# Decoder trunk on one core: the identity products between stages are left out

## The chip, the cores and the metric

The kernel runs on one NeuronCore of one Trainium2 chip. The metric is device time in microseconds (us) of that core, the median of repeated runs. Lower is better.

## The reference

Two layers work on two groups of tokens that share one set of weights: a prompt of 16 meta tokens and 256 prompt tokens, and eight sample sequences of eight tokens. That makes 336 token columns, and the model width is 1024. Each layer has three sub-layers:

```
x = x + 0.5 * rms_norm(swiglu(rms_norm(x, g0), gate1, up1, down1), g1)
x = x +       rms_norm(mixer(rms_norm(x, g2), ...),               g3)
x = x + 0.5 * rms_norm(swiglu(rms_norm(x, g4), gate2, up2, down2), g5)
```

The mixer joins a gated delta-rule head group (four heads of 128) and a short gated convolution into one output projection. All arithmetic is 32-bit floating point. Both a sub-layer's input and its output are normalised, so nothing of the next sub-layer can be multiplied before the output's norm is known and the sum with x has been made.

## The kernel before, in words

Everything is kept features first: a tile holds 128 features on the partitions and up to 336 tokens along the row, and x is eight such tiles. A weight block of 128x128 is split into a high part WH (ScalarE, L710) and a low part WL (VectorE, L1003), x likewise into XH (ScalarE, L727) and XL (VectorE, L1015). Each product of the model is therefore three TensorE products of 336 columns: WH with XH, WH with XL, WL with XH. The helper `three` (L1437 to L1439) issues them; `entry` issues its own (L1477, L1478, L1482). Weights come by DMA into three slots from the sync queue.

The five engines' programs are written by hand, each one a plain sequence, joined by semaphores. A layer is FFN (j = 0), mixer (j = 1), FFN (j = 2). Between two of them lies a hand-over, on which four engines work in turn:

- TensorE, `out_norm(layer, j)`: sums the squares of the output over the features with columns of ones. L1574 does it for the tiles summed so far, L1577 for the last tile. After that it waits for y_inv and spreads the inverse root over the partitions with three transposes (L1455).
- ScalarE takes the root (L767).
- VectorE takes the reciprocal (L1051) and, once TensorE's rows are there, scales the eight output tiles (L1058) and adds them to x (L1064).
- ScalarE then makes XH from each new tile of x (L727), VectorE XL (L1015).
- TensorE's `entry` begins as soon as XH of tile 0 stands. Its first three parts use tiles 0, 1 and 2 of x for three outputs each: 27 products. The rest follow as the tiles come.

The norm of the new x is not needed before the first outputs are read. Its column sums (L1462) stand among TensorE's products, ScalarE takes the root (L752), VectorE the reciprocal (L1027), TensorE spreads it (L1455 again), and VectorE copies it (L1029) and scales the first outputs (L1101, L1102). The products of the third chunk after them wait for that.

There are six hand-overs, the last of them at the end of the program with no stage behind it. In the first five, `out_norm` also calls `keep_busy(n)`: n products of the 128x128 identity with itself into columns of bank 6 of PSUM that nobody reads (L1569). They are issued without a wait of their own. A call with n = 4 (n = 2 for j = 1) stands between L1577 and the wait for y_inv, and a call with n = 7 behind L1455. A 32-bit product of this kind is two passes, each with a weight load, so it makes two records in the profile. At the start of the program 14 products on a blank tile (L1833) are issued in the same way, while the first data are on their way; the change does not touch those.

Of the kernel before, what the change touches and what calls it, by code (L numbers as in the profile page):

```python
# [22 lines left out]
P = 128  # L23
DEPTH = 2
# [228 lines left out]
def decoder_trunk(nc, io):  # L253
    ctx = ExitStack()
    with ctx:
# [16 lines left out]
        def stack(at, *specs):  # L272
            out = []
            for name, shape, dt in specs:
# [47 lines left out]
        (NI, MI), e_end = stack(h_at, ("NI", [P, TT, HEADS, P], F32), ("MI", [P, TT, HEADS, P], F32))  # L322
        (EXT,), at = stack(e_end - size([P, 2 * HEADS, G_LEN]), ("EXT", [P, QKV_T, G_LEN], F32))
        (OH, _, OL), _ = stack(at, ("OH", [P, HEADS, TP], F32R), ("OV", [P, HEADS, TP], F32),
                                  ("OL", [P, HEADS, TP], F32R))
        (QKV, UEXT, ZS, BY, QKM), at = stack(
# [31 lines left out]
        PS = ctx.enter_context(nc.psum_tensor("PS", [P, 8, 512], F32))  # L358
# [56 lines left out]
        def mask(name, width=P):  # L415
            return MK[:, MASKS.index(name), 0:width]
# [59 lines left out]
        def tcols(t):  # L476
            return slice(t * P, (t + 1) * P)
# [516 lines left out]
        def _(dve):  # L994
# [198 lines left out]
            def mixer(layer):  # L1193
                for step in STEPS:
# [81 lines left out]
                    elif what == "mirror":  # L1276

                        _, t, m = step
                        own(("y", t, m), layer)
                        if m < SQUARE:  # L1280
# [5 lines left out]
                        ins.then_inc(mirrored.sem, 1)  # L1286
                    elif what == "x":
                        _, t, m = step
                        group(step, layer)
                        name = "lv8_meta" if t == C_TILE and m == 8 else f"lv{m}"  # L1290
# [143 lines left out]
        def _(pe):  # L1434
# [17 lines left out]
            def rows(col, out):  # L1452

                for t in range(TT):
                    ins = pe.transpose(out[:, tcols(t)], col[:, t:t + 1].to_broadcast([P, P]), mask("ident"))  # L1455
                return ins
# [106 lines left out]
                for m in range(KT):  # L1563
                    down_tile(m)

            def keep_busy(n):

                for _ in range(n):
                    pe.matmul(PS[:, 6, 0:P], mask("ident"), mask("ident"), start=True, stop=True)  # L1569

            def out_norm(layer, j):
                pe.wait_ge(y_acc.sem, y_acc.at(j * (KT - 1) + KT - 2, layer))
                for t in range(TT):
                    pe.matmul(Y_COLS[:, t:t + 1], ACCY[:, tcols(t)], mask("ones", 1), start=(t == 0), stop=False)  # L1574
                pe.wait_ge(y_sq.sem, y_sq.at(j * KT + KT - 1, layer))
                for t in range(TT):
                    ins = pe.matmul(Y_COLS[:, t:t + 1], SQY[(KT - 1) % 2][:, tcols(t)], mask("ones", 1), start=False,  # L1577
                                    stop=(t == TT - 1))
                ins.then_inc(y_cols.sem, 1)
                last = (layer, j) == (DEPTH - 1, 2)  # L1580
                if not last:
                    keep_busy(2 if j == 1 else 4)
                pe.wait_ge(y_inv.sem, y_inv.at(j, layer))
                rows(RC[:, 1, :], Y_ROWS).then_inc(y_rows.sem, 1)
                if not last:
                    keep_busy(7)

            def evacuated(name, layer):

# [244 lines left out]
            for layer in range(DEPTH):  # L1834
                ffn(layer, 0)
                out_norm(layer, 0)
                mixer(layer)
                out_norm(layer, 1)
                ffn(layer, 1)
                out_norm(layer, 2)  # L1840
# [96 lines left out]
```

## Time and profile before

| | us |
|---|---|
| median of 3 runs | 1436.12 |
| lowest and highest run | 1435.62, 1437.96 |
| time of the profiled execution | 1436.65 |
| its span, first to last instruction | 1434.8 |
| TensorE, busy in the span | 1413.1 |
| mean granted clock of TensorE | 0.997 |

The span is what the profile's views divide up; 1.85 us of the profiled execution lie around it. The profiled execution is 0.53 us above the median. In the profile, PE is TensorE's products and PEld its weight loads. A product's end is modelled, so products that follow each other closely overlap in the rows: the distance from start to start is the pace, and the duration of one is longer than that.

### The profile page before, as it was taken

To read this page: it belongs to the slowest core of one execution; us is meant where nothing else is said; L and a number is where in the kernel's file an instruction comes from. 1 tells how busy PE (TensorE), PEld (TensorE's weight loads), DVE (VectorE), ACT (ScalarE), POOL (GpSimd) and SP (SyncE) were. 2 spreads that over 40 slices of the span, in tenths; PEclk is the share of its full clock that TensorE was granted. 3 is DMA by queue.
4 is the path that set the end of the run, shared out by engine and by line. 5 is a ranking of instruction groups with operands and counts; after the bars stand their busy time and mean duration, and the time that the engine had idled before them with its cause. 6 is when DMAs were issued, how large, how long until landed. Compare 5 with 4: busy or idle time off the path is not lost.

```text
span 1434.8 us, 22786 instructions
## 1 busy us (share of the span) xinstructions
PE 1413.1 (98%) x9588; PEld 1397.8 (97%) x9588; DVE 880.0 (61%) x1486; ACT 625.1 (44%) x978; POOL 37.3 (3%) x124
## 2 busy tenths in 40 slices
PE   8999999999999999999999999999999999999997
PEld 8999999899999999999999999998999999999997
DVE  5655533798697765553376555348986967655433
ACT  5444333572444444433344443336734345444332
POOL 0000000110000000000000000001100000000000
PEclk9999999999999999999999999999999999999998
DMA  6544344322116344434435443442221253444442
GB/s 225 208 147 147 120 142 162 107 89 89 65 60 207 115 136 140 146 122 145 163 126 193 137 145 128 144 166 92 89 89 64 71 203 118 149 155 148 138 144 98
DMA packets 49605, 191.17 MB, mean 133 GB/s; under 512 B 6144, under 2 KB 8576, under 8 KB 48992
## 3 DMA queue, kind: packets, MB, share of 16 engines
q1 hardware_dynamic: 48896, 184.60, 38.5%
q0 software_dynamic: 608, 5.12, 0.9%
q8 instruction: 76, 1.25, 0.3%
q14 instruction: 25, 0.20, 0.0%
HBM read 183.27 MB, written 6.43 MB: 132 GB/s over the span
## 4 chain that ended last, share of the span: by engine, by line
PE 91%; DVE 6%; ACT 2%; issue 0%; DMA 0%; SPq 0%; ACTq 0%
PE PS L1437 26%; PE PS L1438 26%; PE PS L1439 26%; PE PS L1608 3%; DVE WL L1003 2%; PE PS L1716 1%; PE PS L1705 1%; PE PS L1477 1%; PE PS L1482 1%; PE PS L1478 1%; ACT XH L727 1%; DVE XL L1015 1%; PE PS L1738 1%; PE PS L1606 1%; DVE X L1064 1%; PE PS L1649 1%
## 5 line engine op out<-in xcount | busy, mean ns | idle before, releaser
L1437 PE MATMUL PS<-XH,WH 128*128 128x336 f32 (+1 forms) x1728 | 550.3, 318 | 2.6 <-DVE WL L1003 2.0
L1439 PE MATMUL PS<-XH,WL 128*128 128x336 f32 (+1 forms) x1728 | 542.3, 314 | 0.0
L1438 PE MATMUL PS<-XL,WH 128*128 128x336 f32 (+1 forms) x1728 | 541.9, 314 | 0.0
L1003 DVE TENSOR_TENSOR WL<-RAW,WH 128x1024 fp32r<-128x1024 f32 (+1 forms) x312 | 398.1, 1300 | 195.4 <-ACT WH L710 195.3
L710 ACT ACTIVATE WH<-RAW 128x1024 fp32r<-128x1024 f32 (+1 forms) x312 | 345.4, 1120 | 255.8 <-DMA RAW<-in_w_down 172.5
L1437 PEld LDWEIGHTS PS<-XH,WH 128*128 128x128 f32 x1728 | 324.7, 188 | 4.2 <-issue 2.9
L1438 PEld LDWEIGHTS PS<-XL,WH 128*128 128x128 f32 x1728 | 324.8, 188 | 0.3
L1439 PEld LDWEIGHTS PS<-XH,WL 128*128 128x128 f32 x1728 | 324.3, 188 | 0.0
L1437 PE MATMUL PS<-HH,WH 128*128 128x336 f32 (+1 forms) x704 | 221.4, 314 | 0.0
L1438 PE MATMUL PS<-HL,WH 128*128 128x336 f32 (+1 forms) x704 | 221.2, 314 | 0.0
L1439 PE MATMUL PS<-HH,WL 128*128 128x336 f32 (+1 forms) x704 | 221.1, 314 | 0.0
L1101 DVE TENSOR_TENSOR GR<-PS,RB 128x336 f32<-128x336 f32 (+1 forms) x88 | 44.3, 503 | 185.0 <-PE PS L1439 184.9
L1437 PEld LDWEIGHTS PS<-HH,WH 128*128 128x128 f32 x704 | 132.5, 188 | 0.0
L783 ACT ACTIVATE HH<-HF 128x336 fp32r<-128x336 f32 (+1 forms) x88 | 42.4, 482 | 206.8 <-DVE HF L1107 206.8
L1438 PEld LDWEIGHTS PS<-HL,WH 128*128 128x128 f32 x704 | 132.2, 188 | 0.0
L1439 PEld LDWEIGHTS PS<-HH,WL 128*128 128x128 f32 x704 | 132.1, 188 | 0.0
L781 ACT ACTIVATE SG<-GR 128x336 f32<-128x336 f32 (+1 forms) x88 | 42.1, 479 | 109.4 <-DVE GR L1101 109.3
L1109 DVE TENSOR_TENSOR HL<-HF,HH 128x336 fp32r<-128x336 f32 (+1 forms) x88 | 44.4, 505 | 48.2 <-ACT HH L783 48.2
L1477 PE MATMUL PS<-XH,WH 128*128 128x336 f32 (+1 forms) x192 | 62.4, 329 | 4.8 <-DVE WL L1003 2.7
L1478 PE MATMUL PS<-XH,WL 128*128 128x336 f32 (+1 forms) x192 | 59.6, 314 | 0.0
L1482 PE MATMUL PS<-XL,WH 128*128 128x336 f32 (+1 forms) x192 | 47.6, 315 | 0.0
L1477 PEld LDWEIGHTS PS<-XH,WH 128*128 128x128 f32 x192 | 36.0, 187 | 10.9 <-DVE WL L1003 4.9
(240 smaller groups left out, 1299.6 us busy)
## 6 DMA issues: line engine op xcount, KB each, us to landing
RAW<-in_w_up SPq DMA_DIRECT2D x176, 512.0 KB, 4.6
RAW<-in_w_down SPq DMA_DIRECT2D x64, 704.0 KB, 4.1
RAW<-in_w_in SPq DMA_DIRECT2D x56, 512.0 KB, 4.6
RAW<-in_w_out SPq DMA_DIRECT2D x16, 512.0 KB, 4.5
SEQ_S<-in_states SPq DMA_DIRECT2D x2, 2048.0 KB, 10.0
out_state_s<-SEQ_S POOLq DMA_DIRECT2D x2, 2048.0 KB, 7.3
X<-in_x SPq DMA_DIRECT2D x8, 168.0 KB, 5.4
out_y<-X SPq DMA_DIRECT2D x4, 320.0 KB, 2.3
```

Source lines behind the costliest of these rows:

```text
L710: act.activation(WH[slot][:, cols], RAW[slot][:, cols], ACT.Copy).then_inc(split_hi.sem, 1)
L783: act.activation(hidden(HH, c, n), HF[k][:, 0:n], ACT.Copy).then_inc(h_hi.sem, 1)
L1003: dve.tensor_tensor(WL[slot][:, cols], RAW[slot][:, cols], WH[slot][:, cols].bitcast(F32), ALU.subtract).then_inc(split_lo.sem, 1)
L1101: dve.tensor_tensor(GR[k][:, 0:n], PS[:, up_bank(c, 0), 0:n], RB[:, 0:n], ALU.mult).then_inc(gate_scaled.sem, 1)
L1109: dve.tensor_tensor(hidden(HL, c, n), HF[k][:, 0:n], hidden(HH, c, n).bitcast(F32), ALU.subtract).then_inc(h_lo.sem, 1)
L1437: pe.matmul(out, wh, xh, start=first, stop=False)
L1438: pe.matmul(out, wh, xl, start=False, stop=False)
L1439: return pe.matmul(out, wl, xh, start=False, stop=last)
L1477: pe.matmul(out, wh, XH[:, kt, 0:n], start=(kt == 0), stop=False)
L1478: pe.matmul(out, wl, XH[:, kt, 0:n], start=False, stop=False)
L1482: ins = pe.matmul(out, wh, XL[:, kt, 0:n], start=False, stop=(kt == KT - 1))
L1608: ins = pe.matmul(out[:, h, :], lhsT(h), rhs(h), start=True, stop=True)
```

## The change

`keep_busy` and its two calls in `out_norm` are deleted. Nothing else differs. The products of the five hand-overs number 11 + 9 + 11 + 11 + 9 = 51.

```diff
-            def keep_busy(n):
-
-                for _ in range(n):
-                    pe.matmul(PS[:, 6, 0:P], mask("ident"), mask("ident"), start=True, stop=True)
-
             def out_norm(layer, j):
...
                 ins.then_inc(y_cols.sem, 1)
-                last = (layer, j) == (DEPTH - 1, 2)
-                if not last:
-                    keep_busy(2 if j == 1 else 4)
                 pe.wait_ge(y_inv.sem, y_inv.at(j, layer))
                 rows(RC[:, 1, :], Y_ROWS).then_inc(y_rows.sem, 1)
-                if not last:
-                    keep_busy(7)
```

TensorE's order at the hand-over from the first FFN of layer 0 to the mixer. MK is the tile of masks, whose first is the identity; RC holds the roots. Before:

```order
L1439 MATMUL PS<-HH,WL_56 128x336
L1574 MATMUL PS<-MK,ACCY 128x1 [waits y_acc]
L1574 MATMUL PS<-MK,ACCY 128x1 x2
L1577 MATMUL PS<-MK,SQY_81 128x1 [waits y_sq]
L1577 MATMUL PS<-MK,SQY_81 128x1 x2
L1569 MATMUL PS<-MK 128x128 x4
L1455 MATMUL PS<-MK,RC 128x128 [waits y_inv]
L1455 MATMUL PS<-MK,RC 128x128 x2
L1569 MATMUL PS<-MK 128x128 x7
L1477 MATMUL PS<-XH,WH_60 128x336 [waits split_lo,x_hi,in_masks]
L1478 MATMUL PS<-XH,WL_57 128x336
```

And with the change, where the two lines of column sums are now L1569 and L1572:

```order
L1439 MATMUL PS<-HH,WL_56 128x336
L1569 MATMUL PS<-MK,ACCY 128x1 [waits y_acc]
L1569 MATMUL PS<-MK,ACCY 128x1 x2
L1572 MATMUL PS<-MK,SQY_81 128x1 [waits y_sq]
L1572 MATMUL PS<-MK,SQY_81 128x1 x2
L1455 MATMUL PS<-MK,RC 128x128 [waits y_inv]
L1455 MATMUL PS<-MK,RC 128x128 x2
L1477 MATMUL PS<-XH,WH_60 128x336 [waits split_lo,x_hi,in_masks]
L1478 MATMUL PS<-XH,WL_57 128x336
```

The four and the seven identity products are gone, and nothing has moved into their place: the same waits follow each other with no work of TensorE's own between them. The other four hand-overs change alike, with two products instead of four ahead of the rows where j = 1. ScalarE, VectorE and the sync queue have the same order as before.

## Rows read from the trace of the kernel before

**Rows 1.** The page, busy time by engine: us (share of the span), instructions

```profile
PE 1413.1 (98%) x9588; PEld 1397.8 (97%) x9588; DVE 880.0 (61%) x1486; ACT 625.1 (44%) x978; POOL 37.3 (3%) x124
```

**Rows 2.** The page, TensorE's granted clock in 40 slices, in tenths

```profile
PEclk9999999999999999999999999999999999999998
```

**Rows 3.** The page, the chain that ended last, by engine

```profile
PE 91%; DVE 6%; ACT 2%; issue 0%; DMA 0%; SPq 0%; ACTq 0%
```

**Rows 4.** The identity products' line: duration of one, min/median/max in ns

```profile
L1569 PE MATMUL PS<-MK x102: 275/275/356, 256.2 to 1186.6; 128*128 128x128 f32 x102
```

**Rows 5.** Timeline, first FFN to mixer: start, us, engine, line, [idle before <-releaser]

```profile
254.62 0.31 PE L1439 MATMUL PS<-HH,WL 128*128 128x336 f32 x1
...
256.16 1.14 PE L1569 MATMUL PS<-MK 128*128 128x128 f32 x8
...
257.21 0.17 DVE L1051 RECIPROCAL RC<-RC 128x3 f32<-128x3 f32 x1
...
257.44 0.54 PE L1455 MATMUL PS<-MK,RC 128*128 128x128 f32 x3
...
257.82 1.73 PE L1569 MATMUL PS<-MK 128*128 128x128 f32 x14
...
259.18 0.58 ACT L727 ACTIVATE XH<-X,PAR_ALL 128x336 fp32r<-128x336 f32 x1 [1.64 <-DVE X L1064]
...
259.90 0.39 PE L1477 MATMUL PS<-XH,WH 128*128 128x336 f32 x1 [0.36 <-ACT XH L727]
```

**Rows 6.** Timeline, the hand-over at the end of layer 0

```profile
721.33 1.14 PE L1569 MATMUL PS<-MK 128*128 128x128 f32 x8
...
721.80 0.18 DVE L1051 RECIPROCAL RC<-RC 128x3 f32<-128x3 f32 x1 [1.37 <-ACT RC L767]
...
722.30 0.49 PE L1455 MATMUL PS<-MK,RC 128*128 128x128 f32 x3
```

**Rows 7.** Windows, the longest and shortest hand-over: us, TensorE busy, clock, DMA

```profile
254.62:259.90 5.28, 4.79 (x40) 1.00 0.57 199
1182.55:1187.19 4.64, 4.33 (x36) 1.00 0.63 224
```

**Rows 8.** Windows of the program's end, from its last wide product on

```profile
1422.89:1426.50 3.61, 2.21 (x18) 1.00 0.00 0
1426.50:1427.00 0.50, 0.00 (x0) 0.65 0.00 0
1427.00:1434.80 7.80, 0.00 (x0) 0.50 0.47 169
```

**Rows 9.** Windows: blank products at the start (L1833), identity products in hand-over 1 (L1569)

```profile
1.10:6.10 5.00, 5.00 (x23) 5.00 (x24) 1.00 0.81 237
257.82:259.40 1.58, 1.58 (x14) 1.53 (x14) 1.00 0.83 337
```

**Rows 10.** The line of the blank products at the start

```profile
L1833 PE MATMUL PS<-TMP x28: 274/421/579, 1.1 to 6.9; 128*128 128x128 f32 x28
```

**Rows 11.** Windows: a stretch of up products; the first 27 products of an entry

```profile
60.00:80.00 20.00, 20.00 (x132) 1.00 0.42 143
474.15:479.06 4.91, 4.83 (x27) 1.00 0.00 2
```

**Rows 12.** Timeline, the norm of x in the mixer's entry, layer 0

```profile
275.73 2.35 DVE L1003 TENSOR_TENSOR WL<-RAW,WH 128x1024 fp32r<-128x1024 f32 x2
...
277.36 0.32 PE L1661 MATMUL PS<-XL,W8X 128*8 128x336 f32 x1
```

**Rows 13.** The same place, TensorE alone

```profile
278.22 0.54 PE L1455 MATMUL PS<-MK,RC 128*128 128x128 f32 x3 [0.54 <-DVE RC L1027]
```

**Rows 14.** Timeline, the norm of x in the second FFN's entry, layer 0

```profile
496.21 0.51 DVE L1029 COPY RB<-PS 128x336 f32<-128x336 f32 x1 [1.80 <-PE PS L1455]
```

**Rows 15.** The same place, TensorE alone

```profile
498.95 0.39 PE L1437 MATMUL PS<-XH,WH 128*128 128x336 f32 x1 [0.47 <-DVE WL L1003]
```

## The prediction

> **What bounds the kernel now.** I read the page first. TensorE is busy for 1413.1 of 1434.8 us [rows 1], and the chain that ended last runs through it for 91% [rows 3]. So two things count: what TensorE has to do, and at which pace. The slices of the granted clock are full but for the last one [rows 2]. Next come the places where the chain leaves TensorE. The first five hand-overs are such places. In each, TensorE's column sums, ScalarE's root, VectorE's reciprocal, TensorE's rows, VectorE's scaling and sum and ScalarE's XH follow one another, and every one waits for the one before. From the start of the last wide product to the start of the first wide product of the next stage this takes 4.64 to 5.28 us [rows 7]; the other three lie between. The identity products fill TensorE's part of that time. The line has 102 records, two for each of 51 products [rows 4], and it is the only thing that the change removes.
>
> **What the removed work holds up.** In the hand-over from the first FFN to the mixer [rows 5], the eight passes ahead of the rows begin at 256.16, and the rows (L1455) only at 257.44, which is 0.06 us after VectorE's reciprocal has ended (257.21 + 0.17 = 257.38). The fourteen passes behind the rows begin at 257.82 and last 1.73 us, to 259.55. XH of the first tile ends at 259.18 + 0.58 = 259.76, and the first product of the mixer comes at 259.90 after 0.36 us of idle time. So neither group is waited for: both lie beside ScalarE and VectorE. Four of the five hand-overs read like this. One does not [rows 6]: its reciprocal ends at 721.98, and the rows begin at 722.30, straight behind the identity passes and with no idle time before them. With 0.06 us from reciprocal to rows, as there, they could begin at 722.04. The change gives **0.26 us** there and nothing in the other four. Were these 102 records all on the path, the gain would be about 102 x 0.11 us, but [rows 5] exclude that.
>
> **What the removed work may have given.** The granted clock has two levels, 2.4 GHz (1.00) and 1.2 GHz (0.50). The trace shows one fall. From 1422.89, the start of the last wide product, TensorE had only column sums of one column and the three rows of the last hand-over, where no identity products stand. The clock is at 1.00 up to 1426.50 and at 0.65 on average in the half microsecond behind that, so it fell 3.8 us after the last wide product's start [rows 8]. The other five hand-overs run through the same column sums and rows, take 4.64 to 5.28 us, and show 1.00 all the way [rows 7]; what they have besides are the identity products. Without them, each looks to the clock like the end of the program, and each is longer than the 3.8 us after which it fell there. I expect falls.
>
> The Trainium skill (TensorE: Matmul & The Clock Gate, section "Why this matters for your kernels") says that idle gaps of a few microseconds between bursts of products send the clock back to its lower level. That rule speaks against this change, and the trace agrees as far as [rows 8] go: one fall, in a stretch like that.
>
> **What a fall costs.** At the lower level a product takes twice as long. The start shows how long that can last. The blank products run at 5.00 / 23 = 0.217 us a pass, the identity products in the hand-over at 1.58 / 14 = 0.113 [rows 9]; so the start was at the lower level, though the view prints 1.00 there, having no record yet. The blank passes run from 1.1 to 6.9 us, and only the last are short (median 421 ns, minimum 274) [rows 10]. So it took up to 5.8 us of steady work for the clock to rise. For the slow working time s of one hand-over, the bounds are 0 (no fall, or a fall that ends before the first wide product) and 5.8 us. No row shows a rise in an entry. The entry's products are wider than the blank ones, and follow each other more closely, so I put s nearer the middle than the upper end: 2.9 us. TensorE loses half of s: 1.45 us.
>
> Part of that is covered. A product of 336 columns takes 20.00 / 132 = 0.152 us [rows 11]. The first 27 of an entry need 27 x 0.152 = 4.10 us and take 4.91, since the tiles of x come only every 1.6 us; so 0.81 us of idle time is there to be used up. Leaves 1.45 - 0.81 = **0.64 us**.
>
> What is late next differs. Where an FFN follows (three hand-overs), VectorE's copy L1029 has waited 1.80 us for TensorE's rows [rows 14], and TensorE in turn waits at 498.95 for what VectorE does after it [rows 15]. Everything is passed on, and 0.64 us stays. Where the mixer follows (two hand-overs), TensorE's last product before the rows of x's norm starts at 277.36 and would end its turn at 277.51, but the rows come at 278.22, because VectorE is held by the weight split L1003 until 278.08 [rows 12, 13]. This is a cover of 0.71 us, and 0.64 fits under it.
>
> **The sum.** The fall is not tied to the program, and the work ends 0.8 to 1.5 us after the point at which it fell at the end [rows 8]; so I count it at two of the three costly hand-overs: 2 x 0.64 = 1.28 us, less 0.26, makes +1.0 us. Against the profiled execution (1436.65 us, span 1434.8 and 1.85 around it) this is 1437.7; that execution is 0.53 above the median, so against the median of 1436.12 I predict **1437.1 us**. A measurement of this kernel can tell about 0.2%, 2.9 us, from no change. At the lower end, s = 0 everywhere: -0.26, 1435.9. At the upper end, s = 5.8 everywhere: half is 2.9, less 0.81 is 2.09; three times that is 6.27; the mixer's two, less 0.71, are 2 x 1.38 = 2.76; less 0.26 is +8.8, 1444.9.
>
> The same page (section "Terms") prices a throttled stretch at its length times one minus the share of clock passed, and subtracts no cover. By it, five stretches of 2.9 us would cost 5 x 2.9 x 0.5 = 7.25 us.
>
> **The rivals.**
>
> *The clock comes back late.* One mechanism, in the entries: TensorE falls in each hand-over and stays slow for as long as at the start. For it: [rows 10] are the only rise in the trace. Against it: the blank passes were narrow. It decides from s = 3.4 us on: half is 1.72, and 3 x (1.72 - 0.81) + 2 x (1.72 - 0.81 - 0.71) - 0.26 = +2.9 us, the bound. In the middle between 3.4 and 5.8, with half at 2.3, it is 3 x 1.49 + 2 x 0.78 - 0.26 = +5.8, 1441.9 us. This ends on the slower side.
>
> *No cover.* The fall is as in the forecast, but in all five hand-overs, and the idle time does not absorb it, because each tile's products must be done before the next tile's can make up for them. 5 x 1.45 - 0.26 = +7.0, 1443.1 us. Against it: the pauses [rows 11] lie right among the slow products.
>
> *The clock holds.* The rows and column sums, with their weight loads, are enough to keep it, or the fall comes too late to matter. Then -0.26 us, 1435.9. Against it: [rows 8].
>
> *The identity products are in the way.* The change makes the kernel faster by over 2.9 us. That needs 0.58 us in each of five hand-overs; [rows 5] show 0.06 us between reciprocal and rows, and 0.36 us of idle time ahead of the first product.
>
> That the change does not do what it says is excluded: the order printed above shows the products gone and nothing in their place.
>
> **How the numbers follow.** Forecast (falls, small cost) 0.50; clock holds 0.18; late return 0.23; no cover 0.05; in the way 0.04. The first two are within 0.2%: 0.68. Late return and no cover are slower by more: 0.28. Faster by more than 0.2%: 0.04. The range runs from 1435.6 (no fall, at the lowest run shown) to 1442.0, the middle of the late return, and leaves out the upper half of that, no cover and the faster case, about 2 in 10.
>
> **What would show it.** In the changed kernel: no L1569 with identity operands; in the hand-over at the end of layer 0, rows 0.06 us after the reciprocal; granted clock at 0.50 in stretches at the end of the hand-overs or in the first microseconds of the entries, and L1477 with starts about 0.30 us apart there; the first 27 products of an entry taking 5.5 us rather than 4.91; the mixer's rows at the same distance from the reciprocal as before. A clock of 1.00 throughout would make the forecast wrong, as would stretches at 0.50 of 4 us and more of work.

## The result, and the profile after

| us | before | with the change |
|---|---|---|
| median | 1436.18 | 1439.57 |
| lowest to highest, 20 runs each | 1435.33 to 1437.96 | 1437.53 to 1442.45 |
| span of the profiled execution | 1434.8 | 1437.6 |
| mean granted clock | 0.997 | 0.987 |

The ratio is 1.0025, with a 95% interval of 1.0018 to 1.0032: slower by 3.4 us, a little over the 2.9 us that I called the bound of no change. It is also less even: the 20 runs spread over 4.9 us instead of 2.6, and the five whose mean granted clock was 0.984 or 0.985 took 1441.11 to 1442.45 us, while 14 of the 15 with 0.986 to 0.988 took 1440.48 or less.

The page of the changed kernel, busy time by engine, granted clock and the chain that ended last:

```profile
PE 1405.4 (98%) x9486; PEld 1395.2 (97%) x9486; DVE 880.3 (61%) x1486; ACT 625.2 (43%) x978; POOL 37.4 (3%) x124
...
PEclk9999999999999999999999999999999999999998
...
PE 94%; DVE 4%; ACT 1%; DMA 0%; issue 0%; SPq 0%
```

TensorE has 102 records fewer and is busy for 7.7 us less than in [rows 1], and yet the span is 2.8 us longer. The slices of the clock look as in [rows 2]: a tenth of full speed is too coarse for a fall inside a slice of 36 us. The chain tells more. Against [rows 3], TensorE's share of it has grown from 91 to 94% and VectorE's has shrunk from 6 to 4%: the path now stays on TensorE where it used to wait for the others.

The view by windows, cut where the clock changes, shows all of it (us, TensorE busy with records, clock, DMA share, GB/s). Here are the low stretch at each of the five hand-overs and, for the first, its neighbours:

```profile
250.00:257.71 7.71, 6.53 (x46) 1.00 0.64 201
257.71:264.53 6.82, 4.93 (x18) 0.50 0.16 65
264.53:270.00 5.47, 5.47 (x37) 1.00 0.00 0
...
472.75:479.57 6.82, 5.29 (x19) 0.50 0.20 82
...
725.33:732.16 6.83, 6.15 (x22) 0.50 0.08 34
...
977.92:981.33 3.41, 2.85 (x10) 0.50 0.03 13
...
1189.55:1192.96 3.41, 2.93 (x11) 0.50 0.14 50
```

The clock falls to 1.2 GHz (0.50) in every hand-over. TensorE's busy time in each stretch is the slow working time s of the prediction: 4.93, 5.29, 6.15, 2.85 and 2.93 us. The timeline of the first hand-over shows what it does to the products (start us, us):

```profile
257.13 0.54 PE L1455 MATMUL PS<-MK,RC 128*128 128x128 f32 x3 [1.14 <-DVE RC L1051]
259.60 0.62 PE L1477 MATMUL PS<-XH,WH 128*128 128x336 f32 x1 [1.93 <-ACT XH L727]
260.02 0.48 PE L1478 MATMUL PS<-XH,WL 128*128 128x336 f32 x1
260.30 0.48 PE L1477 MATMUL PS<-XH,WH 128*128 128x336 f32 x1
...
264.67 0.31 PE L1477 MATMUL PS<-XH,WH 128*128 128x336 f32 x1
264.82 0.32 PE L1478 MATMUL PS<-XH,WL 128*128 128x336 f32 x1
```

The first product follows the rows by 2.47 us, as in [rows 5] (259.90 less 257.44 is 2.46), so the idle stretch costs nothing by itself. Then products start 0.28 us apart, not 0.15, until the rise at 264.53. What becomes of the lost time, in the hand-over to the second FFN of layer 0:

```profile
474.28:480.91 6.63, 6.63 (x28) 0.60 0.01 2
480.91:488.27 7.36, 7.36 (x51) 1.00 0.01 2
488.27:494.71 6.44, 6.44 (x45) 1.00 0.63 217
```

The first 27 products take 6.63 us instead of the 4.91 of [rows 11]: 1.72 us late. The products of the next two stretches, the second of which ends at the column sums of the new x, lay in the trace of the kernel before at

```profile
479.06:486.62 7.56, 7.56 (x48) 1.00 0.01 2
486.62:493.17 6.55, 6.55 (x43) 1.00 0.64 211
```

They took 7.56 and 6.55 us and now take 7.36 and 6.44, so 0.31 us more is made good, and 1.41 us stays for good. The whole account, from the start of the same instruction in both traces (hand-over 3 has its 0.22 us of gain at the rows already taken off):

| hand-over, next stage | s, us | lateness added, us |
|---|---|---|
| 1, mixer | 4.93 | 0.44 |
| 2, FFN | 5.29 | 1.41 |
| 3, FFN | 6.15 | 1.31 |
| 4, mixer | 2.85 | 0.00 |
| 5, FFN | 2.93 | -0.01 |
| sum | 22.15 | 3.15 |

The changed kernel's trace came into the first hand-over 0.31 us ahead of the other one's, which leaves the 2.84 us between the spans.

### The profile page after: what moved, and what is told of

It reads as the page before. It is cut to its first block, busy times and chain, and to the rows that moved or that the text cites. A ratio compares the mean times of both kernels' runs of the same rounds, so it can differ in the third digit from the quotient of the medians.

```text
span 1437.6 us, 22582 instructions
## 1 busy us (share of the span) xinstructions
PE 1405.4 (98%) x9486; PEld 1395.2 (97%) x9486; DVE 880.3 (61%) x1486; ACT 625.2 (43%) x978; POOL 37.4 (3%) x124
## 4 chain that ended last, share of the span: by engine, by line
PE 94%; DVE 4%; ACT 1%; DMA 0%; issue 0%; SPq 0%
PE PS L1437 26%; PE PS L1438 26%; PE PS L1439 26%; PE PS L1598 3%; PE PS L1477 2%; PE PS L1478 2%; PE PS L1482 2%; PE PS L1706 1%; PE PS L1695 1%; DVE WL L1003 1%; PE PS L1728 1%; PE PS L1596 1%; PE PS L1639 1%; ACT XH L727 0%; DVE X L1064 0%; PE PS L1455 0%
## 5 line engine op out<-in xcount | busy, mean ns | idle before, releaser
L1437 PEld LDWEIGHTS PS<-XH,WH 128*128 128x128 f32 x1728 | 324.7, 188 | 4.2 <-issue 2.9
L1477 PEld LDWEIGHTS PS<-XH,WH 128*128 128x128 f32 x192 | 40.1, 209 | 14.1 <-issue 10.6
```

The lines of the kernel that those rows point to most:

```text
L1437: pe.matmul(out, wh, xh, start=first, stop=False)
L1477: pe.matmul(out, wh, XH[:, kt, 0:n], start=(kt == 0), stop=False)
```

## Experiments

The account says that the loss is the clock's, that a fall is paid only where it outlasts what the entry can make good, and that the hand-overs to an FFN pay most of it. Eight kernels test this. Each was timed in 10 or 11 runs beside 32 or 33 of the kernel before, whose median was 1436.39 in both sets. Each edit is against the kernel before.

**Only the group behind the rows.**

```diff
-                if not last:
-                    keep_busy(2 if j == 1 else 4)
```

> Only the products behind the rows are kept (7 in each of the first five hand-overs); the 4 or 2 ahead of the rows are left out. Theory (all the change's loss is TensorE's clock, and the identity products only keep it up): the 14 passes fill 1.6 us of the 4.6 to 5.3 us, so the clock falls in fewer hand-overs than the five of the changed kernel, and the time lies below the changed kernel's, about +0 to +1.5 us to the kernel before; in the hand-over at the end of layer 0 the rows follow the reciprocal by 0.06 us, 0.26 earlier. Rival (both groups are needed): falls in all five and about +3 us. Rival (the loss is not the clock but TensorE's restart after an idle stretch): the gap behind the rows stays filled, so -0.3 us whatever the clock does.

Measured: 1436.62 us, ratio 1.0000 (0.9991 to 1.0009). The time is as the theory has it, but not for its reason. The clock fell in four of the five hand-overs, once each for 3.4 us. In the windows of this kernel's trace:

```profile
257.23:260.65 3.42, 3.14 (x15) 0.50 0.57 217
472.27:475.69 3.42, 3.42 (x18) 0.50 0.57 210
974.03:977.45 3.42, 3.42 (x17) 0.50 0.32 128
1185.66:1189.07 3.41, 3.41 (x18) 0.50 0.43 171
```

And in its timeline, in the first of them:

```profile
257.51 0.90 PE L1455 MATMUL PS<-MK,RC 128*128 128x128 f32 x3 [1.14 <-DVE RC L1051]
258.20 2.90 PE L1569 MATMUL PS<-MK 128*128 128x128 f32 x14
260.85 0.40 PE L1477 MATMUL PS<-XH,WH 128*128 128x336 f32 x1
261.09 0.32 PE L1478 MATMUL PS<-XH,WL 128*128 128x336 f32 x1
```

The fall comes ahead of the rows. The rows take 0.90 us instead of 0.54, the fourteen passes take 2.90 us instead of 1.73, and the entry begins 0.9 us late. But the rise comes at 260.65, ahead of the first wide product, which finds the full clock. Of the 0.9 us the entry makes 0.54 good; the 0.34 us that the slow rows cost stays, as VectorE waits for them. The second hand-over keeps 0.23 us in the same way, the fourth and the fifth nothing, though there the lower clock still reached 1.2 us into the wide products; the third has its gain of 0.22 us. The group behind the rows does not keep the clock up here; it moves most of the slow time to where there is no other work. The rival that both groups are needed for the time falls, since its +3 us lies outside the interval. That of a cost of restarting is not decided by this time: its -0.3 us lies inside.

**Only the group ahead of the rows.**

```diff
-                if not last:
-                    keep_busy(7)
```

> Only the products ahead of the rows are kept (4, or 2 where j = 1); the 7 behind the rows are left out, and they lie directly ahead of the entry. Theory (clock): 8 or 4 passes are less work than 14, so more falls than with the group behind alone: three to five of the hand-overs, and about +1.5 to +3 us to the kernel before. Rival (one group is as good as the other): the same time as with the group behind alone. Rival (restart after an idle stretch): the full +3 us, with entries late from their first product on and a granted clock of 1.00.

Measured: 1439.54 us, ratio 1.0019 (1.0010 to 1.0028), +3.15. That is the changed kernel's time. Five falls, all over wide products:

```profile
259.92:263.33 3.41, 3.41 (x13) 0.50 0.00 0
474.96:478.37 3.41, 3.41 (x14) 0.50 0.00 0
724.13:730.96 6.83, 5.80 (x21) 0.50 0.11 43
976.72:983.54 6.82, 5.81 (x21) 0.50 0.05 16
1191.76:1195.17 3.41, 3.41 (x13) 0.50 0.00 0
```

With the group ahead alone, nothing is gained over having none; the fall only comes later, in three of five after the entry has begun. The two groups are not alike, and the restart rival falls: the granted clock is not 1.00, and in the first hand-over the first wide product follows the rows by 2.46 us, as in the kernel before. From the same instructions in both traces, the five hand-overs added 0.0, 0.56, 1.63, 0.87 and 0.38 us. The first two compare well: each had 3.41 us of unbroken products at the lower clock, and the one ahead of the mixer cost nothing where the one ahead of the FFN cost 0.56. The fourth shows that a hand-over to the mixer pays as well once the slow work is long: 5.81 us of it cost 0.87.

**Products only where an FFN follows.**

```diff
-                if not last:
+                if not last and j > 0:
```

(at both calls)

> Identity products only in the three hand-overs that an FFN follows (j = 1 and j = 2); none in the two that the mixer follows. Theory: there the clock falls, the entry runs late by 1 to 2 us, but the wait for the norm of x behind it covers about 0.7 us, so of two falls about 0 to 1 us is left: +0.0 to +1.0 us to the kernel before, within its measurement. Rival (no cover): two falls at half of about 4 us each, +4 us.

Measured: 1437.46 us, ratio 1.0006 (0.9997 to 1.0015), +1.07, at the theory's upper end; the +4 us of the rival lies outside the interval. Its trace has two falls, at the two hand-overs without products:

```profile
260.43:263.85 3.42, 3.42 (x14) 0.50 0.00 0
973.82:980.65 6.83, 5.01 (x18) 0.50 0.19 76
```

The first added 0.0 us and the second 0.5. The clock held at the three others. The cover behind the mixer's entry is real: 5.01 us of slow work left 0.5 us here, and 5.29 us ahead of an FFN left 1.4 in the changed kernel.

**Products only where the mixer follows.**

```diff
-                if not last:
+                if not last and j == 0:
```

(at both calls)

> Identity products only in the two hand-overs that the mixer follows (j = 0); none in the three that an FFN follows. Theory: the loss of the changed kernel sits here, since nothing behind the entry covers it: +2 to +3.5 us to the kernel before, less 0.26 for the rows at the end of layer 0. Rival (the loss is spread evenly over the five hand-overs): three fifths of 3.4 us, +2.0 us, and the kernel with products only ahead of an FFN at +1.4 us.

Measured: 1439.83 us, ratio 1.0023 (1.0015 to 1.0032), +3.44. As much as the whole change. Three falls, at the three hand-overs without products:

```profile
473.21:480.04 6.83, 5.81 (x21) 0.50 0.11 47
725.80:729.21 3.41, 3.28 (x12) 0.50 0.02 10
1186.60:1193.42 6.82, 4.95 (x19) 0.50 0.31 117
```

An even spread would have given +2.0 here and +1.4 in the kernel above; the interval here, +2.1 to +4.6 us, lies above the first, the other does not decide. With +1.07 and +3.44, the two halves come to 4.5 us where the change has 3.4. The runs of such kernels spread over some 4 us, so the difference of 1.1 is not one that I can read anything from.

**Two products ahead of the rows everywhere.**

```diff
-                    keep_busy(2 if j == 1 else 4)
+                    keep_busy(2)
```

> Two products instead of four ahead of the rows in the three hand-overs behind an FFN, so two everywhere; seven behind, as before. Theory: the rows at the end of layer 0 come 0.26 us earlier, and the clock falls seldom, since the two hand-overs at j = 1 held it with two: -0.3 to +0.5 us to the kernel before. Rival (the group of four is needed where j is not 1): falls in three hand-overs, each short, +0.5 to +1 us.

Measured: 1436.29 us, ratio 0.9999 (0.9990 to 1.0008), -0.1. The clock was at 1.00 from 6.68 to 1426.62, and the rows at the end of layer 0 follow the reciprocal directly, unlike in [rows 6]:

```profile
721.68 0.18 DVE L1051 RECIPROCAL RC<-RC 128x3 f32<-128x3 f32 x1 [1.64 <-ACT RC L767]
721.91 0.54 PE L1455 MATMUL PS<-MK,RC 128*128 128x128 f32 x3
```

0.05 us lie between them, where there were 0.32. The gain of some 0.2 us is there in the trace and too small for the timing. No fall came in the hand-overs where two products stood in place of four, so the rival falls.

**Twice the products.**

```diff
-                    keep_busy(2 if j == 1 else 4)
+                    keep_busy(4 if j == 1 else 8)
...
-                    keep_busy(7)
+                    keep_busy(14)
```

> Twice the identity products: 8 (4) ahead of the rows, 14 behind. Theory (they are free only inside the waits): at full clock a pass takes 0.113 us, so 16 passes ahead run 0.53 us beyond the place of the rows at j = 0 and 0.9 us beyond it in the hand-over at the end of layer 0, and 28 passes behind end 1.1 us or more behind the first tile's XH; the entries start 1.5 us late or more, of which 0.8 us and the mixer's 0.7 us are made good: +3 to +5 us, with the clock at 1.00 throughout. Rival (more of them costs nothing, since TensorE catches up in the entry): within 1 us of the kernel before.

Measured: 1438.65 us, ratio 1.0016 (1.0007 to 1.0024), +2.3, at a clock of 1.00 from 5.21 to 1428.57. The products are free only inside the waits, as the theory has it; the price is lower than the +3 to +5 us that I said, though its interval reaches +3.4. At the end of layer 0:

```profile
723.28 3.29 PE L1569 MATMUL PS<-MK 128*128 128x128 f32 x28
...
724.62 0.57 ACT L727 ACTIVATE XH<-X,PAR_ALL 128x336 fp32r<-128x336 f32 x1 [2.15 <-DVE X L1064]
...
726.32 0.40 PE L1477 MATMUL PS<-XH,WH 128*128 128x336 f32 x1
```

XH stands at 725.19, and the entry begins 1.1 us later. This kernel loses nothing to the clock, so it shows lateness and its cover by themselves. From the same products in both traces, the rows of the five hand-overs came 0.59, 0.27, 0.89, 0.59 and 0.27 us late, 2.6 us together, because the group ahead of them was still running; the first wide products came 1.50, 1.21, 1.88, 1.50 and 1.24 us late. Behind the entries 0.57, 0.23, 0.89, 0.58 and 0.23 us were left, 2.5 together. So what the rows are late is paid whole, as every engine behind them waits. The 0.9 to 1.0 us that the group behind the rows adds is made good whole, in the entry's pauses. My expectation had 0.8 us made good, and 0.7 more ahead of the mixer. But the mixer's cover did nothing here: 0.57 and 0.58 us were left in its two hand-overs, all that their rows had been late.

**Three products behind the rows, none ahead.**

```diff
-                if not last:
-                    keep_busy(2 if j == 1 else 4)
...
-                    keep_busy(7)
+                    keep_busy(3)
```

> Three products behind the rows, none ahead. Theory (what counts is that the clock is back up when the first wide product comes): six passes are too little work for that, so falls last into the entries as in the changed kernel: +2.5 to +3.5 us. Rival (any work in the gap is enough): as with seven behind the rows, +0.2 us.

Measured: 1438.05 us (1436.30 to 1441.11 over its ten runs), ratio 1.0013 (1.0004 to 1.0023), +1.7. Between the two expectations, and its interval, +0.6 to +3.3 us, reaches into the theory's. Its trace has three falls, over 3.5, 3.2 and 4.1 us of wide products, and none in two hand-overs. Neither side was right. The spread is the widest in this study next to the changed kernel's own, and the two slowest of its runs have the lowest mean granted clock (0.985, against 0.990 to 0.993 in the four fastest), which suggests that it is a matter of the single execution.

**Seven products behind the rows, only where an FFN follows: 21 instead of 51.**

```diff
-                if not last:
-                    keep_busy(2 if j == 1 else 4)
...
-                if not last:
+                if not last and j > 0:
                     keep_busy(7)
```

> Seven products behind the rows in the three hand-overs that an FFN follows, none elsewhere: 21 products instead of 51. Theory: the loss of leaving the mixer's two out is about that of the kernel with products ahead of an FFN alone (+1.07 us, one fall of 3.4 us and one of 6.8 in its trace), and leaving out the groups ahead of the rows costs +0.2: about +1.2 us. Rival (with the group behind alone the short falls add up): +2.5 us.

Measured: 1437.17 us, ratio 1.0004 (0.9995 to 1.0013), +0.8. Near the theory, and the rival's +2.5 lies outside the interval. The five windows at 0.50 in its trace:

```profile
8.37:11.78 3.41, 3.41 (x13) 0.50 1.01 305
257.54:264.37 6.83, 4.93 (x19) 0.50 0.20 81
472.58:476.00 3.42, 3.42 (x18) 0.50 0.44 171
974.34:981.17 6.83, 6.14 (x22) 0.50 0.03 9
1185.97:1189.38 3.41, 3.41 (x17) 0.50 0.45 179
```

The first lies at the start of the program. The two long ones lie in the hand-overs to the mixer, end far into its entry, and added 0.40 and 1.0 us. The two short ones lie in hand-overs to an FFN and reach 1.3 and 1.4 us into the wide products, which the entries make good. None of the eight kernels is shown to be faster than the kernel before; the one with two products ahead and the one with the group behind alone cannot be told from it.

## Why the prediction was right, and where it was not

The measured median lies inside the range, and the mechanism is the forecast's: falls, slow products, a part of them made good. The forecast's own case did not come. It had +1.0 us, inside the bound of 2.9, and the result is beyond that bound, among the outcomes that had 0.28; and the prediction itself named stretches with 4 us and more of work at the lower clock as a sign against it, of which there were three. That the range held is owed to the late-return rival, up to whose middle it was drawn.

- *The removed passes are waited for in one place, 0.26 us.* Right. The changed kernel makes up 0.22 us there, and nothing in the other four. The two-ahead kernel shows the same.
- *The clock will fall.* Right, and in all five hand-overs, where I had let two of the three costly ones count. The fall at the program's end [rows 8] was the right model for the rest.
- *The slow working time is 2.9 us.* This is the term that was mis-sized. In the changed kernel's trace it was 4.93, 5.29, 6.15, 2.85 and 2.93 us, a mean of 4.4, and one value lies above the 5.8 us that I had as the upper end. I had put it at the middle because an entry's products are wider and closer than the blank ones at the start. No row supported the step from there to an earlier rise. The rival that had the clock come back late decided from 3.4 us on; this is what happened in three hand-overs of five, and it is nearer to the result than my forecast is.
- *A slow product takes twice as long.* Nearly: 0.28 us against 0.152, so a slow microsecond loses 0.46 us and not 0.5.
- *The entry makes 0.81 us good.* Too little. In hand-over 2, 5.29 us at 0.46 are 2.4 us lost and 1.4 left: 1.0 us was made good, since pauses behind the first 27 products count too (0.31 us). The doubled products, with 0.9 to 1.0 us made good at the full clock, fit that.
- *The mixer's 0.71 us of cover.* Right. In hand-over 1, 4.93 x 0.46 is 2.3, less 1.0 is 1.3, less 0.71 is 0.6; it was 0.44. In the mixer's stage TensorE's last product before the rows then starts at 278.29 and the rows at 278.44: the cover is used up, where there was idle time [rows 13]. Hand-over 4 paid nothing.
- *The sum.* +1.0 foretold, +3.4 measured, inside the range and outside the forecast's own case. With the measured s, 0.46 and 1.0 in place of my three figures, the five hand-overs come to 0.6, 1.4, 1.6, 0 and 0.3 us, 3.9 together, against 3.15 in the trace, a little too high in the first, third and fifth. In the third they are right behind the entry, where 1.57 us had been added; 0.26 us came back further on in the stage. Steps of that size show in other traces too, away from any hand-over (1.71 us of lateness to 1.46 between the second and the third where products stand ahead of the mixer only), so I read nothing from differences below 0.3 us. With the measured s alone and my other two figures it would be +5.4 us, so those two were off the other way.

The three new figures and the s of the windows can be held against three kernels from which none of them was taken. Lateness added behind each entry, in us, without the gain at the rows:

| kernel, hand-overs | by the three figures | in the trace |
|---|---|---|
| group ahead alone, 1 to 5 | 0, 0.6, 1.7, 1.0, 0.6 | 0.0, 0.6, 1.6, 0.9, 0.4 |
| products only ahead of an FFN, 1 and 4 | 0, 0.6 | 0.0, 0.5 |
| products only ahead of the mixer, 2, 3 and 5 | 1.7, 0.5, 1.3 | 1.6, 0.5, 0.8 |

They fit but for the fifth hand-over, which they put too high here as in the changed kernel. Why it pays less is open.

What the chance of 0.68 for "no change" rested on was that one middle value. The Trainium skill (TensorE: Matmul & The Clock Gate, section "Terms") prices all time at the lower clock at one minus the share of clock passed, without a cover. An estimate by it is 13.7 us for the 27.3 us of the five stretches, or 11.1 us if only their 22.15 us of work are counted; the trace has 3.15. The cover is the larger part of the difference: at 0.46 the 22.15 us of slow work lose 10.2 us, and 6.8 of these were made good in the entries and ahead of the mixer's rows.

What stays open: what decides in a single execution whether a stretch lasts 3.4 or 6.8 us. Hand-overs of the same form had the one in one trace and the other in another; with the group ahead of the rows alone, 3.4 us in hand-over 1 and 6.8 in hand-over 4. I did not try to control it.

## What to carry to other kernels

Before removing idle-time products, find the place in the trace where the same wait stands without them: here it was the program's last hand-over, and it foretold the fall. A fall of the clock is then priced by how much of the useful work it overlaps, less the pauses behind it that can be made up, so the same 3.41 us of slow products cost 0.56 us ahead of an FFN and nothing ahead of the mixer. Where filler is wanted, try it right ahead of the work that must be fast, and inside the wait: the seven products that stood there did as well as all eleven, the other four (or two) alone did nothing, three in the place of the seven left +1.7 us, and twice as much cost 2.3 us, by the trace all of it from the part ahead of a step that the other engines wait for. How much of this is the place and how much the number is not shown. The pair nearest in number is 15 products behind the rows (+1.7 us) and 16 ahead of them (+3.15), and their intervals overlap.

## What the runs showed of the hardware that I had not expected

- The clock also fell after TensorE had gone back to work. With the group ahead of the rows alone, it fell at 259.92, 0.1 us after the first wide product of the mixer's entry at 259.83, and at 474.96, 0.9 us after that of the second FFN's, and each time stayed down for 3.41 us of unbroken products.
- Every low stretch between two full ones, in all these traces (27 of them), lasted 3.41 or 6.83 us; there was none between.
- The start of the program can fall as well, without any difference in its code: in the last kernel above, the clock was low from 8.37 to 11.78, behind the first wait for weights, and in none of the other traces.
